# Four of eleven down tiles of the first block's feed-forwards as seven block products each, behind the up tiles

## What is computed

```python
D_MODEL = 1024
SEQ = 256
DEPTH = 2
D_FF = 2816
FFN_RES_WEIGHT = 0.5
...
def swiglu_ffn(x, w1, w2):
    a, b = jnp.split(x @ w1, 2, axis=-1)
    return (jax.nn.silu(a) * b) @ w2
...
x = x + FFN_RES_WEIGHT * swiglu_ffn(rms_norm(x, ffn1_norm[l]), ffn1_w1[l], ffn1_w2[l])
...
x = x + FFN_RES_WEIGHT * swiglu_ffn(rms_norm(x, ffn2_norm[l]), ffn2_w1[l], ffn2_w2[l])
```

## Time and profile before

| | |
|---|---|
| median of 3 runs | 2240.15 us (2240.14 to 2240.87) |
| the profiled execution's own time | 2240.4 us |
| its span in the profile | 2238.7 us |
| mean granted TensorE clock | 0.999 |
| busy: TensorE, weight loads, VectorE, ScalarE | 99%, 85%, 68%, 54% of the span |

### The profile page before, as it was taken

The page is one execution under the profiler, slowest core; times in us unless marked ns, Lnnn a source line. Parts: engine busy times, 40 slices in busy tenths (PEclk is TensorE's granted clock), DMA queues, the critical chain, the costliest instruction groups (busy, mean ns, idle before and its releaser), DMA issues.

```text
span 2238.7 us, 30449 instructions
## 1 busy us (share of the span) xinstructions
PE 2222.5 (99%) x12350; PEld 1898.8 (85%) x12350; DVE 1529.8 (68%) x2112; ACT 1210.0 (54%) x1812; POOL 67.6 (3%) x118
## 2 busy tenths in 40 slices
PE   8999999999999999999999999999999999999998
PEld 7888987888888889878888988888888988888887
DVE  6557578665665575786656866786777766786766
ACT  6456455454564564555545655455555555455554
POOL 0000000000000000000000200000000100000000
PEclk9999999999999999999999999999999999999999
DMA  8565544455545655434655544445555544445553
GB/s 286 192 232 184 199 180 151 171 188 188 188 186 190 232 186 204 182 144 169 232 189 190 187 151 165 156 153 181 190 192 178 189 151 165 156 166 181 188 188 113
DMA packets 62803, 409.38 MB, mean 183 GB/s; under 512 B 7976, under 2 KB 9512, under 8 KB 15304
## 3 DMA queue, kind: packets, MB, share of 16 engines
q1 hardware_dynamic: 62664, 407.44, 50.5%
HBM read 405.83 MB, written 2.10 MB: 182 GB/s over the span
## 4 chain that ended last, share of the span: by engine, by line
PE 94%; DVE 3%; ACT 1%; DMA 1%; issue 0%; SPq 0%; POOLq 0%; DVEq 0%; POOL 0%; ACTq 0%
PE bank L593 20%; PE bank L594 20%; PE bank L595 20%; PE bank L640 18%; PE bank L647 9%; DVE w_lo L270 1%; PE bank L393 1%; PE bank L1733 1%; PE bank L1745 1%; DMA w_raw<-in_tiles 0%; PE bank L2345 0%; PE bank L2052 0%; PE bank L2513 0%; PE bank L2062 0%; PE bank L2072 0%; PE bank L2532 0%
## 5 line engine op out<-in xcount | busy, mean ns | idle before, releaser
L270 DVE TENSOR_TENSOR w_lo<-w_raw,w_hi 128x2048 fp32r<-128x2048 f32 x367 | 835.1, 2284 | 69.0 <-ACT w_hi L240 68.6
L240 ACT ACTIVATE w_hi<-w_raw 128x2048 fp32r<-128x2048 f32 x359 | 685.3, 1912 | 107.7 <-DMA w_raw<-in_tiles 107.5
L640 PE MATMUL bank<-hT,w_hi 128*128 128x512 f32 x1920 | 459.5, 390 | 2.4 <-DVE w_lo L270 2.4
L640 PEld LDWEIGHTS bank<-hT,w_hi 128*128 128x128 f32 x1920 | 355.8, 188 | 73.8 <-DVE w_lo L270 2.8
L593 PE MATMUL bank<-w_hi,hT 128*128 128x512 f32 (+2 forms) x832 | 327.9, 394 | 0.3
L595 PE MATMUL bank<-w_hi,hT 128*128 128x512 f32 (+2 forms) x832 | 318.9, 383 | 0.0
L594 PE MATMUL bank<-w_lo,hT 128*128 128x512 f32 (+2 forms) x832 | 318.8, 383 | 0.0
L647 PEld LDWEIGHTS bank<-hT,w_lo 128*128 128x128 f32 x1920 | 247.7, 191 | 10.3
L647 PE MATMUL bank<-hT,w_lo 128*128 128x256 f32 x1920 | 250.9, 283 | 0.0
L593 PEld LDWEIGHTS bank<-w_hi,hT 128*128 128x128 f32 x832 | 156.8, 188 | 37.6 <-issue 7.9
L595 PEld LDWEIGHTS bank<-w_hi,hT 128*128 128x128 f32 x832 | 156.6, 188 | 31.3
(11 more groups left out here) (395 smaller groups left out, 2984.8 us busy)
## 6 DMA issues: line engine op xcount, KB each, us to landing
w_raw<-in_tiles SPq DMA_DIRECT2D x368, 1024.0 KB, 4.8
a_cmp_w<-in_cmp_w SPq DMA_DIRECT2D x2, 2048.0 KB, 7.8
shifted<-in_bias SPq DMA_DIRECT2D x12, 256.0 KB, 7.2
w_raw<-in_tiles SPq DMA_DIRECT2D x8, 256.0 KB, 5.7
a_gm_rows<-in_rows SPq DMA_DIRECT2D x2, 768.0 KB, 7.0
x_res<-in_x SPq DMA_DIRECT2D x2, 512.0 KB, 5.1
a_ret_rows<-in_rows SPq DMA_DIRECT2D x2, 512.0 KB, 8.0
b_rows<-in_rows SPq DMA_DIRECT2D x2, 512.0 KB, 6.2
```

What stands on the lines that cost most here:

```text
L240: act.activation(k.hi[slot][:], k.raw[slot][:], ACT.Copy).then_inc(k.hi_done[slot], 1)
L270: dve.tensor_tensor(k.lo[slot][:], k.raw[slot][:], k.hi[slot][:].bitcast(F32), ALU.subtract).then_inc(k.lo_done[slot], 1)
L640: pe.matmul(bank[:], k.hi[slot][:, w], k.hT[:, c].rearrange("p a s -> p (a s)"), start=c == 0, stop=False)
```

## The change

The order of the tiles is now made by a class `Plan`. For the first block's feed-forwards (`GATED`), down tiles 0 and 1 stay where they were. Down tiles 2 to 8 (`tail`) wait until all up tiles are done and then run in the order 2, 6, 3, 7, 4, 5, 8; 9 and 10 follow as before. Tiles 2, 3, 4 and 5 (`strassen`) are done as seven block products in place of eight. That takes, for each of the four:

- sums of the activation blocks, written to `sums` by `add_blocks` (four 128 x 128 operations of VectorE), rounded by ScalarE (`sums_hi`) and completed by VectorE (`sums_lo`, 128 x 512);
- differences of the weight blocks, which VectorE makes with `make` (one operation of 128 x 1024, two of 128 x 512, each waiting for the one before) in a slot of their own of the ring; this made tile is rounded and completed like one that was loaded, but is not loaded;
- seven products in `strassen`. Three add to `acc`; four gather in banks 0 to 3, which the up tiles have left by then, over all four tiles.

Behind the last of them `recombine` adds the four banks to `x` in eight operations of VectorE, after one copy by ScalarE. The split activations of pairs 2 to 8 are kept in buffers `z_hi` and `z_lo`, since they are used later. The second block's feed-forwards (`CONVOLVED`) keep their order. The join has one more statement, which completes tile `end` behind the first addition; before, that tile was completed ahead of the join.

```diff
+    def make(self, dve, m, link):
+        k, slot, made = self.k, self.slot[m], self.slot[m + 1]
+        w = k.raw[slot][:].rearrange("p (c n e) -> p c n e", c=2, n=2)
+        t = k.raw[made][:].rearrange("p (q e) -> p q e", q=4)
+        dve.wait_ge(k.landed[slot], 16 * self.nth[m])
+        dve.wait_ge(k.used[made], self.before[m + 1])
+        link(dve.tensor_tensor(t[:, 0:2], w[:, :, 1], w[:, 0], ALU.subtract))
+        link(dve.tensor_tensor(t[:, 2], w[:, 1, 1], t[:, 0], ALU.subtract))
+        dve.tensor_tensor(t[:, 3], w[:, 1, 0], t[:, 2], ALU.subtract).then_inc(k.landed[made], 16)
...
+        self.order = [("up", 0, 0), ("up", 0, 1)]
+        for i in range(1, FFN_PAIRS):
+            self.order += [("up", i, 0), ("up", i, 1)]
+            if i - 1 not in tail + ENDING:
+                self.order.append(("down", i - 1))
+        for i in tail + ENDING:
+            self.order.append(("down", i))
+            if i in strassen:
+                self.order.append(("made", i))
...
+GATED = Plan((2, 3, 4, 5), (6, 7, 8), (2, 6, 3, 7, 4, 5, 8))
+CONVOLVED = Plan((), (), ())
...
+        ring.ready(pe, n)
+        product(self.acc[0][0], a12, n, 2, False, False)
+        product(self.acc[0][1], s4, n, 3, False, False)
+        ring.ready(pe, n + 1)
+        product(self.acc[1][0], a22, n + 1, 3, False, False)
+        if first:
+            pe.wait_ge(self.summed[0], self.parts(FFN_PAIRS - 1, 1))
+        product(k.bank[2], s2, n + 1, 2, first, last)
+        product(k.bank[3], s3, n + 1, 1, first, last)
+        if first:
+            pe.wait_ge(self.summed[1], self.parts(FFN_PAIRS - 1, 1))
+        product(k.bank[0], a11, n, 0, first, last).then_inc(k.used[ring.slot[n]], 1)
+        product(k.bank[1], s1, n + 1, 0, first, last).then_inc(k.used[ring.slot[n + 1]], 1)
...
                 k.ring.hi_to(act, self.up_at(i, j) + SLOTS - 1)
...
+                if j == 0 and i - 1 in self.plan.strassen:
+                    self.sums_hi(act, i - 1)
+                if self.conv is None and j == 0 and i == FFN_PAIRS - 1:
+                    k.ring.hi_to(act, self.up_at(i, 1) + SLOTS - 1)
...
+                if self.plan.strassen and (i, j) == (FFN_PAIRS - 2, 1):
+                    ring.make(dve, self.down_at(self.plan.strassen[0]), link)
                 self.convolve(dve, i, j)
                 self.add_parts(dve, i, j, 1)
+                if self.plan.strassen and (i, j) == (FFN_PAIRS - 1, 1):
+                    ring.make(dve, self.down_at(self.plan.strassen[1]), link)
+                if j == 0 and i - 1 in self.plan.strassen:
+                    self.add_blocks(dve, i - 1, link)
                 self.combine(dve, i, j)
                 self.split_lo(dve, i, j)
+                if j == 1 and i - 1 in self.plan.strassen:
+                    self.sums_lo(dve, i - 1, link)
...
+        for i in self.plan.strassen[1:]:
+            if i != self.plan.strassen[1]:
+                ring.lo_to(dve, self.down_at(i))
+                ring.make(dve, self.down_at(i), link)
+            ring.lo_to(dve, self.down_at(i) + 2)
+        ring.lo_to(dve, self.end)
+        if self.plan.strassen:
+            self.recombine(dve, link)
```

More of the change, by code:

```diff
@@ L268, in lo_to @@
             slot = self.slot[m]
+            if m + 1 < len(self.places) and self.places[m + 1] is None:
+                dve.wait_ge(k.landed[self.slot[m + 1]], 16 * self.nth[m + 1])
             dve.wait_ge(k.hi_done[slot], self.nth[m])
@@ L423, in vector @@
         self.add(dve, 0)
+        ring.lo_to(dve, self.end + 1)
         norm.vector_xn(dve, 0)
@@ L706, in up @@
         if i == 1 and j == 1:
-            for first_ok in self.first_ok:
-                pe.wait_ge(first_ok, self.which + 1)
+            pe.wait_ge(self.first_ok, NT * (self.which + 1))
         last = i == FFN_PAIRS - 1
@@ L752, in down, with activations, strassen, product @@
         return last
+    def activations(self, i, t, j):
+        if i in self.plan.later:
+            return self.z_hi[i][:, 2 * j + t], self.z_lo[i][:, 2 * j + t]
+        ts = slice(t * P, (t + 1) * P)
+        return self.g_hi[i % 2][j][:, ts], self.g_lo[i % 2][j][:, ts]
+    def strassen(self, pe, i):
+        k, ring, n = self.k, self.k.ring, self.down_at(i)
+        a11, a12, a22, s1, s2, s3, s4 = range(7)
+        first, last = i == self.plan.strassen[0], i == self.plan.strassen[-1]
+        def product(bank, block, tile, q, start, stop):
+            w, slot = slice(q * 512, (q + 1) * 512), ring.slot[tile]
+            return three_passes(pe, bank[:], (self.z_hi[i][:, block], self.z_lo[i][:, block]),
+                                (k.hi[slot][:, w], k.lo[slot][:, w]), start, stop)
+        ring.ready(pe, n)
[11 more added lines that the diff above has]
+        product(k.bank[1], s1, n + 1, 0, first, last).then_inc(k.used[ring.slot[n + 1]], 1)
     def tensor(self, pe, following):
@@ L765, in tensor @@
                     self.turn(pe, 1)
-            if i < N - 1:
-                k.ring.ready(pe, self.down_at(i - 1))
-                for j in range(2):
-                    pe.wait_ge(self.glo_done[j], self.base + i)
-                    for t in range(NT):
-                        last = self.down(pe, i - 1, t, j)
-                last.then_inc(used(i - 1), 1)
+            if i - 1 not in self.plan.tail + ENDING:
+                self.whole(pe, i - 1)
+        if self.plan.strassen:
+            pe.wait_ge(self.chain, self.links + 4 * len(self.plan.strassen))
+        for i in self.plan.tail:
+            if i in self.plan.strassen:
+                self.strassen(pe, i)
+            else:
+                self.whole(pe, i)
         if following is None or following.by_columns:
@@ L785, in tensor, with whole @@
                     last.then_inc(used(i), 1)
+    def whole(self, pe, i):
+        k = self.k
+        k.ring.ready(pe, self.down_at(i))
+        for j in range(2):
+            pe.wait_ge(self.glo_done[j], self.base + i + 1)
+            for t in range(NT):
+                last = self.down(pe, i, t, j)
+        last.then_inc(k.used[k.ring.slot[self.down_at(i)]], 1)
     def end_by_columns(self, pe, following):
@@ L865, in split_hi @@
         act.wait_ge(self.g_done[j], self.base + i + 1)
+        if i in self.plan.tail:
+            out, g = self.parts_of(self.z_hi, i, j)
+            act.activation(out, g, ACT.Copy).then_inc(self.ghi_done[j], 1)
+            return
         if i >= 2:
-            self.k.ring.wait_used(act, self.down_at(i - 2), 1)
+            before = max(h for h in range(i) if h % 2 == i % 2 and h not in self.plan.tail)
+            self.k.ring.wait_used(act, self.down_at(before), 1)
         act.activation(self.g_hi[i % 2][j][:], self.g[j][:], ACT.Copy).then_inc(self.ghi_done[j], 1)
@@ L878, in vector @@
         ring.lo_to(dve, self.n0 + SLOTS + 1)
+        link = Link(dve, self.chain)
+        link.n = self.links
         for i in range(1, FFN_PAIRS):
@@ new lines, in vector, with add_blocks @@
+        if self.block_end:
+            ring.lo_half(dve, self.end, 0)
+    def add_blocks(self, dve, i, link):
+        n = self.plan.strassen.index(i)
+        (a11, a21), (a12, a22) = ([g[:, t * P:(t + 1) * P] for t in range(NT)] for g in self.g)
+        s1, s2, s3, s4 = (self.sums[n % 2][:, q] for q in range(4))
+        for j in range(2):
+            dve.wait_ge(self.g_done[j], self.base + i + 1)
+        dve.tensor_tensor(s1, a21, a22, ALU.add)
+        link(dve.tensor_tensor(s3, a11, a21, ALU.subtract))
+        link(dve.tensor_tensor(s2, s1, a11, ALU.subtract))
+        link(dve.tensor_tensor(s4, a12, s2, ALU.subtract))
```

106 lines of the change are left out of this document (79 added, 27 removed).

## The result

The changed kernel takes 2266.05 us (median of 4 runs, 2265.32 to 2267.42), the kernel before 2240.26 beside it: 1.0116 times as long, 95% interval 1.0104 to 1.0129. The profiled executions differ by 24.8 us of span (2238.7 and 2263.5). Slower was right, and so was the place; the forecast of 18 us more fell 7.7 us short.

The account below looks back on a forecast made before the run. TensorE's matmuls were taken to bound the kernel. Per feed-forward 6.6 us of waits plus 0.2 at the join less 2.7 gained, 4.1; four times 16.4, plus the block join, 18.1 over 2240.4: 2258 us, range 2246 to 2267.

Parts of the forecast that it names:

- the forecast of 18 us more: Whole kernel: waits and joins outweigh the matmuls saved, 18.1 us more than before, 2258 us.
- The gain: Seven-product tiles on TensorE: three matmuls fewer each, 0.68 us a tile, 2.7 a feed-forward, 10.9 us in all.
- Pairs 3 to 8 at nothing: Up-tile pairs 3 to 8: TensorE's work hides VectorE's block sums, priced at nothing; uncovered, up to 0.5 us a pair.
- The waits of a feed-forward, 6.6 us: TensorE waiting for VectorE's queue: 3.3 us in tile 2, 0.8 twice at tile 3, 1.7 in two parts later.
- The rival of the clock: TensorE's clock halves in the 3.3 us wait, costing 0.5 to 3.8 us; total 2260 to 2273 us; chance 0.12.
- 0.1 to 0.4 us later, I take 0.2: Join after a feed-forward: tile `end`, 2.20 us, where VectorE idled 1.79, delays it 0.1 to 0.4 us, taken as 0.2.
- 1.9 us once: Join between the blocks: VectorE begins its chain 2.0 us late, costing 1.9 us once.
- the upper end of the range, 2267: Whole kernel: `make` at 3.0 us and VectorE's other steps 2% longer, 2.1 us more a feed-forward, give 2267 us.

Follow-up runs that it names:

- experiment 12: Against the changed kernel: only tiles 2 and 3 seven-product, order 6, 7, 2, 5, 3, 4, 8, recombine ahead of tile 10's remainder, `end` completed before joins; 2234.91 us.
- experiment 4: Changed kernel with tail order 6, 2, 7, 3, 4, 5, 8, so a plain tile first, and each `make` later; 2258.23 us, 1.0080 of the kernel before.
- experiment 5: Changed kernel with VectorE's second addition ahead of a remainder in pair 10's second half; 2269.99 us, 1.0130 of the kernel before.
- experiment 1: Changed kernel with the norm's scaling on VectorE ahead of tile `end`'s remainder in the join; 2269.25 us, 1.0129 of the kernel before.
- experiment 2: Changed kernel with its order of tiles alone, no made or seven-product tile; 2244.74 us, 1.0020 of the kernel before.

## Why the prediction was right, and where its size was off

**The gain** holds: 0.68 us for each tile, seen bare in experiment 12.

**Pairs 3 to 8 at nothing** holds: from the first feed-forward's first transposes to the end of pair 10 the starts of TensorE's matmuls are 0.3 us over their usual distances in all.

**The waits of a feed-forward, 6.6 us**, were right in size. The fourth feed-forward shows them bare: 3.2 in tile 2, 1.4 at tile 3, 1.3 at tile 5 (from start to start, less the usual 0.23), 5.9 us in all; with rests of 0.5, 6.4. The first has 3.2, 1.9 of slow matmuls, 1.3: 6.4. That they are the length of VectorE's queue, and not the order at tile 2, is shown by experiments 4 and 5: with a plain tile first the wait of 3.1 us is gone, and the loss falls only by what VectorE idles less (1.5 and 1.55 us); 0.76 us more of idle time cost 0.8 to 0.9.

**The rival of the clock** was given 0.12 and a price of 0.5 to 3.8 us for a feed-forward. Its condition came true: the clock fell in three of four feed-forwards. Its price didn't; up to the next norm the fall cost nothing that shows. The first feed-forward of the change, where it fell, and that of experiment 1, where it did not, have the addition of the first join at the same distance from the transposes of the first pair, within 0.02 us (165.35 and 165.37). Forecast and rival weren't alternatives: the fall filled time that TensorE would have waited anyway. Behind the block's join, where nothing waits behind it, a fall cost 0.9 us; in experiment 4, with a wait of 2.6 us there and no fall, nothing was lost behind it. That the measured time lies in this rival's 2260 to 2273 too is no sign for it.

**The step that was mis-sized is the joins.** "0.1 to 0.4 us later, I take 0.2" was 1.3 us three times. The sum laid the remainder's 2.20 us over VectorE's 1.79 us of idle time and took the answer it idled for, GpSimd's, as fixed; it was delayed by the very work put there (experiments 1 and 2). And "1.9 us once" at the block's join was 3.0, with 0.9 of slow matmuls behind it: the loads of tiles 9 and 10 held VectorE for 1.28 + 1.48 us where I counted 1.7, and its chain to the scaling took 5.66 us instead of the earlier trace rows's 5.34:

```profile
1244.54 2.29 DVE L274 TENSOR_TENSOR w_lo<-w_raw,w_hi 128x2048 fp32r<-128x2048 f32 x1 [1.28 <-ACT w_hi L242]
1248.31 2.29 DVE L274 TENSOR_TENSOR w_lo<-w_raw,w_hi 128x2048 fp32r<-128x2048 f32 x1 [1.48 <-ACT w_hi L242]
...
1262.74 0.51 DVE L517 TENSOR_SCALAR a_xn<-a_xn,x_double 128x512 f32<-128x512 f32 x1 [0.46 <-POOL x_double L604]
```

The 0.46 us in the last row are the joins' mechanism once more: GpSimd's step L604 took 0.98 us beside a VectorE product of two SBUF inputs that had begun 0.14 us ahead of it (1261.73, 1261.59), and 0.57 in the kernel before, where it began ahead of that product (1238.72, 1238.79).

With 0.6 us at the start, which differs by up to 0.8 us between the experiments, this makes 4 x (6.4 - 2.7) + 3 x 1.3 + 3.0 + 0.9 + 0.6 = 23.2 of the spans' 24.8 us. Most of the rest is two things: the 0.3 us ahead of tile 2, in each feed-forward, and 0.6 us behind the last matmul (7.1 us to the end of the span, 6.5 before). What makes the second is open, and so is the one us more between the medians.

**How near it was.** The time lies 1 us below the upper end of the range, 2267. That end had been set for a slower `make` (3.0 us) and for VectorE's other steps 2% longer, and neither came: `make` takes 2.65 us and a remainder 2.28. The joins, which it didn't provide for, took the room left for these; that it held is luck.

## What to carry to other kernels

A trade of matmuls for work on another engine is priced on that engine's queue over the whole stretch, its idle time included. The waits it makes appear wherever TensorE first reaches the queue's end; in experiment 4 another order of the tiles moved them and took away only what it spared VectorE in idle time. Take as many such tiles as the queue has room for: four lost 25.8 us, and still 17 us in the later order; two, in that order and with recombine early, gained 5.3. Two in the change's own order were not run. Idle time before a join isn't free room: ask which engine's answer it waits for, and whether the work you put there slows that answer.
